# Nine gathered rows for every eight value tiles instead of ten, rows ahead of activations, and two value tiles loaded early, in a one-layer encoder kernel

## What is computed

```python
def _peer(h, w_q, subkeys, u_tab, v_tab):
    q = (xt @ w_q).reshape(t, PEER_HEADS, 2, PEER_QDIM // 2)
    scores = jnp.einsum('thpd,hpkd->thpk', q, subkeys)
    ...
    experts = jnp.take_along_axis(cand_i, sel, axis=-1)   # 128 picks a token
    gates = jax.nn.softmax(top_s, axis=-1)
    def block(args):
        xb, eb, gb = args
        act = jax.nn.gelu(jnp.einsum('tkd,td->tk', u_tab[eb], xb), approximate=False)
        return jnp.einsum('tk,tkd->td', (gb * act), v_tab[eb])

h = _layer_norm(ALPHA * h + mix, ln1_g, ln1_b)
h = _layer_norm(ALPHA * h + ffn, ln2_g, ln2_b)
```

## Time and profile before

| | us |
|---|---|
| three runs | 1959.45, 1963.38, 1967.93 |
| median | 1963.38 |
| the profiled execution | 1959.66 |
| its span, first to last instruction | 1957.9 |
| TensorE busy | 1913.0 (98%) |
| VectorE busy | 1346.7 (69%) |
| GpSimd busy | 1402.1 (72%) |
| ScalarE busy | 986.1 (50%) |

### The profile page before, as it was taken

How to read it: one execution, slowest core, us unless ns; L and a number is a source line. 1 busy time by engine, 2 the same in 40 slices (tenths; PEclk the granted TensorE clock), 3 DMA queues, 4 the chain that set the end, 5 groups by cost and what they waited for, 6 DMA issues and landing times.

```text
span 1957.9 us, 34249 instructions
## 1 busy us (share of the span) xinstructions
PE 1913.0 (98%) x10830; PEld 1670.2 (85%) x10830; DVE 1346.7 (69%) x2302; ACT 986.1 (50%) x1518; POOL 1402.1 (72%) x962
## 2 busy tenths in 40 slices
PE   9999999998999999999999999999899999999996
PEld 8999888888998888888888888888788878778884
DVE  1744012214688878755899989997788888888866
ACT  4544434435445556566455544455455554555553
POOL 6877878886878889898788778784666666566101
PEclk9999999999999999999999999999999999999998
DMA  9555657567869888677877777776899999989881
GB/s 296 172 151 166 205 153 222 180 209 184 207 153 203 186 192 190 167 186 186 248 174 172 177 169 175 170 172 226 317 331 344 340 329 348 366 330 341 298 297 68
DMA packets 178777, 440.59 MB, mean 225 GB/s; under 512 B 27328, under 2 KB 38464, under 8 KB 160912
## 3 DMA queue, kind: packets, MB, share of 16 engines
q1 hardware_dynamic: 163280, 384.52, 68.0%
q0 software_dynamic: 14416, 50.61, 7.4%
q10 hardware_dynamic: 1008, 4.52, 0.6%
HBM read 426.79 MB, written 12.78 MB: 225 GB/s over the span
## 4 chain that ended last, share of the span: by engine, by line
PE 67%; POOL 10%; issue 8%; DMA 7%; DVE 4%; ACT 2%; SPq 2%; DVEq 1%; POOLq 0%; ACTq 0%
PE ps L1771 22%; PE ps L1729 14%; PE ps L1730 7%; PE ps L1469 6%; PE ps L1471 6%; PE ps L1470 6%; POOL u_lo L1398 6%; DMA v_raw<-in_peer_v 4%; POOL w_lo L1360 4%; PE ps L1711 3%; DMA u_raw<-in_peer_u 2%; DVE u_t L1040 1%; DVE v_lo L1265 1%; DVE far_sum L1250 1%; PE ps L1585 1%
## 5 line engine op out<-in xcount | busy, mean ns | idle before, releaser
L1398 POOL TENSOR_TENSOR u_lo<-u_t,u_hi 128x512 fp32r<-128x512 f32 x512 | 653.0, 1300 | 127.4 <-ACT u_hi L637 124.8
L1729 PE MATMUL ps<-xT,u_hi 128*128 128x512 f32 x2048 | 723.0, 397 | 0.5 <-POOL u_lo L1398 0.4
L1730 PE MATMUL ps<-xT,u_lo 128*128 128x256 f32 x2048 | 571.2, 279 | 0.0
L1360 POOL TENSOR_TENSOR w_lo<-raw,w_hi 128x1024 fp32r<-128x1024 f32 x174 | 430.9, 2490 | 110.0 <-ACT w_hi L506 101.1
L637 ACT ACTIVATE u_hi<-u_t 128x512 fp32r<-128x512 f32 x512 | 320.9, 632 | 350.1 <-DVE u_t L1040 349.9
L1729 PEld LDWEIGHTS ps<-xT,u_hi 128*128 128x128 f32 x2048 | 384.3, 188 | 88.2 <-issue 0.9
L1040 DVE STREAM_TRANSPOSE u_t<-u_raw 128x512 f32<-128x512 f32 x512 | 354.1, 700 | 94.7 <-PE ps L1730 51.1
L1730 PEld LDWEIGHTS ps<-xT,u_lo 128*128 128x128 f32 x2048 | 386.1, 189 | 0.0
L506 ACT ACTIVATE w_hi<-raw 128x1024 fp32r<-128x1024 f32 x175 | 184.8, 1059 | 277.7 <-PE ps L1471 258.8
L1771 PE MATMUL ps<-v_hi,m_hi 128*128 128x512 f32 (+1 forms) x896 | 280.4, 380 | 18.1 <-DVE m_lo L1269 11.3
L1771 PE MATMUL ps<-v_hi,m_lo 128*128 128x512 f32 (+1 forms) x896 | 276.5, 376 | 0.0
(11 more groups left out here) (224 smaller groups left out, 2659.3 us busy)
## 6 DMA issues: line engine op xcount, KB each, us to landing
u_raw<-in_peer_u SPq DMA_DIRECT2D x512, 256.0 KB, 4.8
v_raw<-in_peer_v SPq DMA_DIRECT2D x126, 1024.0 KB
raw<-in_w_in SPq DMA_DIRECT2D x111, 512.0 KB, 3.7
raw<-in_w_out SPq DMA_DIRECT2D x32, 512.0 KB, 3.8
raw<-in_w_peer_q SPq DMA_DIRECT2D x128, 128.0 KB, 5.5
act_dram<-act_w ACTq DMA_DIRECT2D x4, 1024.0 KB, 6.7
act_dram<-far_act SPq DMA_DIRECT2D x64, 64.0 KB, 5.1
x_again<-in_x SPq DMA_DIRECT2D x1, 2048.0 KB, 8.0
```

Source lines behind the costliest of these rows:

```text
L1360: pool.tensor_tensor(w_lo[:, k, :], raw[:, k, :], w_hi[:, k % HI_RING, :].bitcast(F32), ALU.subtract).then_inc(lo_done, 1)
L1398: pool.tensor_tensor(u_lo[:, r, :], u_t[:, r, :], u_hi[:, r, :].bitcast(F32), ALU.subtract).then_inc(ulo_done, 1)
L1729: pe.matmul(acc, u_hi[:, r, c], xT[:, :, kt, :], start=kt == 0, stop=False)
L1730: ins = pe.matmul(acc[:, 0:T], u_lo[:, r, c], xT_hi[:, kt, :], start=False, stop=kt == KT - 1)
```

## The change

Four things are done.

1. The first norm's gain and shift are loaded in four halves of 0.5 MB, one behind every second step of the last `w_out` group, and no longer between the subkeys and the query weights.
2. The picks go nine for every eight tiles: five in one four of tiles, four in the next. They run from tile 8 to tile 121. GpSimd first gathers five rows, then asks for the gates, then gathers nine activations; after that one row and one activation in turn. The indices are loaded without waiting for the far stores; VectorE waits for the gates alone (`gate_in`). A row has to wait until the row four (or, for a part of the slots, five) before it is added.
3. Tiles 126 and 127 are loaded as four halves beside value tiles 74 to 77, and are split by ScalarE and VectorE between tiles 120 and 123. `ln2g_sb` is loaded behind tile 125, the last value load.
4. For the last four tiles TensorE takes 126, 127, 124, 125 in each bank. ScalarE and VectorE split half 0 of 124 and 125 first, then half 1 of both.

```diff
-S_CHUNK, S_FIRST = 5, 2
+S_CHUNK, S_FIRST = (5, 4), 2
+S_PAIR = sum(S_CHUNK)
+S_SLOTS = S_CHUNK[0]
...
+            for k in range(STEPS):
+                load_step(O_END - 1, k, w_out[0], (O_END - 1 - B_END) * COL)
+                if k % 2:
+                    dst, row, c = (ln1g_sb, ln1_g, half_row(k // 2)) if k < 4 else (ln1b_sb, ln1_b, half_row(k // 2 - 2))
+                    sp.dma_start(dst[:, c], row[0:1, c].to_broadcast([P, HALF])).then_inc(ln1_rows_in, 16)
...
-            sp.dma_start(ln1g_sb[:], ln1_g[0:1, :].to_broadcast([P, D])).then_inc(ln1_rows_in, 16)
-            sp.dma_start(ln1b_sb[:], ln1_b[0:1, :].to_broadcast([P, D])).then_inc(ln1_rows_in, 16)
...
+                elif n < 10:
+                    t, h = divmod(n - 6, 2)
+                    sp.dma_start(v_late_raw[:, n - 6, :], v_rows[P - 2 + t][:, half_row(h)]).then_inc(v_late, 16)
...
             for s in range(4):
-                v_high(P // 4 - 1, s, 1, last=True)
+                v_high(P // 4 - 2, s, 1)
+                if s % 2 == 0:
+                    v_high_late(s // 2)
+            act.wait_ge(far_added, 1)
+            for s in range(2):
+                act.wait_ge(v_in[s], P // 4 * 16)
+                act.activation(v_hi_end[:, 2 * s, :], v_raw[:, 2 * s, :], ACT.Copy).then_inc(v_hi_done, 1)
+                m_high(m_hi4[:, s, :], P - 4 + s, 1, m_hi_done)
+            for s in range(2):
+                act.activation(v_hi_end[:, 2 * s + 1, :], v_raw[:, 2 * s + 1, :], ACT.Copy).then_inc(v_hi_done, 1)
...
+            def row_gather(k):
+
+                n, j = divmod(k, S_PAIR)
+                if j >= S_SLOTS:
+                    pool.wait_ge(row_added, k - S_SLOTS + 1)
+                elif n:
+                    pool.wait_ge(row_added, k - S_CHUNK[1] + 1)
...
             pool.wait_ge(spread_mm, P - U_SPREAD)
             pool.wait_ge(hot_done, P - U_SPREAD)
+            pool.dma_start(sp_at[:].rearrange("p s k -> p (s k)"), at_dram).then_inc(picks_in, 16)
+            pool.wait_ge(near_out, 64)
+            pool.wait_ge(picks_in, 16)
+            pool.wait_ge(uparts_free, UR + 4 * P)
+            for k in range(S_SLOTS):
+                row_gather(k)
             for s in range(2):
                 pool.wait_ge(far_out[s], 16 * P // 4)
...
-            act_gather(0)
-            act_gather(1)
-            for n in range(S_END):
-                row_gather(n)
-                if n + 2 < S_END:
-                    act_gather(n + 2)
+            pool.dma_start(sp_gate[:], gate_dram).then_inc(gate_in, 16)
+            for k in range(S_PAIR):
+                act_gather(k)
+            for k in range(S_SLOTS, P):
+                row_gather(k)
+                if k - S_SLOTS + S_PAIR < P:
+                    act_gather(k - S_SLOTS + S_PAIR)
...
-                    for s in range(4):
-                        if a == 0 and b % 2 == 0:
-                            pe.wait_ge(v_lo_done, 2 * (P - 4 + s) + b // 2 + 1)
-                        ins = v_products(s, b // 2, a, last=True, stop=s == 3, cs=(b % 2,))
+                    for s in (2, 3, 0, 1):
+                        if a == b == 0 and s >= 2:
+                            pe.wait_ge(late_lo, s - 1)
+                        elif a == 0 and b % 2 == 0 and s < 2:
+                            pe.wait_ge(v_lo_done, 2 * (P - 4) + b + s + 1)
+                        ins = v_products(s, b // 2, a, last=True, stop=s == 1, cs=(b % 2,))
```

More of the change, by code:

```diff
@@ L1256, in weights, with m_low @@
                 dve.tensor_tensor(sp_w[:, k], sp_w[:, k], sp_gate[:, k], ALU.mult)
[L1258 to L1263 removed]
+            def m_low(ml, mh, i, half, done):
+                dve.tensor_tensor(by_four(ml), tile_w(half, i - P // 2 * half), by_four(mh.bitcast(F32)), ALU.subtract).then_inc(done, 1)
@@ L1278, in _, with v_low_added @@
             dve.memset(far_sum[:], 0.0)
[L1279 removed]
+            dve.wait_ge(gate_in, 16)
             for s in range(4):
                 v_low(1, s, 0)
[L1283 to L1286 removed]
+            def v_low_added(n, h, half):
+                weights(n, h, S_CHUNK[h])
                 for s in range(4):
[L1288 removed]
@@ L1301, in _ @@
-            dve.scalar_tensor_tensor(far, far, float(ALPHA), far_sum[:], ALU.mult, ALU.add).then_inc(far_added, 1)
-            for ii in range(S_FIRST + S_END, P // 4 - 1):
-                for s in range(4):
-                    v_low(ii, s, 1)
-            for s in range(4):
-                v_low(P // 4 - 1, s, 1, last=True)
+                    v_low(S_FIRST + n * 2 + h, s, half, added=[(n, h * S_CHUNK[0] + c) for c in range(S_CHUNK[h]) if c * 4 // S_CHUNK[h] == s])
+            for half in range(2):
+                with dve.Fori(half * (S_PAIRS // 2), (half + 1) * (S_PAIRS // 2)) as n:
+                    for h in range(2):
+                        v_low_added(n, h, half)
```

179 lines of the change are left out of this document (88 added, 91 removed).

## The result

| kernel | median us | lowest to highest | before beside it | ratio, 95% interval |
|---|---|---|---|---|
| changed | 1938.18 | 1934.55 to 1941.25 (4 runs) | 1965.22 | 0.9866 [0.9836, 0.9895] |
| changed, again | 1940.82 | 1935.10 to 1948.13 (6 runs) | 1965.52 | 0.988 [0.9858, 0.9902] |

What follows compares the result with a forecast made beforehand. TensorE's own work was taken as the value stretch's bound, with 26 us above it winnable by order. Gains of 5.2 + 5.0 + 1.0 + 7.6 = 18.8 off 1959.66, plus 3.7, gave 1944.6 us, range 1936 to 1955.

Steps and rivals of the forecast that it cites:

- The seam: Before the first query matmuls: moving the first norm's gain rows brings subkeys and TensorE sooner, with clock 5.2 us gained.
- The start: Tile 8 of the value stretch: rows gathered before activations remove wait, slow clock and restart, 6.5 less 1.5, net 5.0.
- The crowding: Value tiles 2 to 4: early rows sharing DMA delay tile 2, late far stores delay the gates; 1.5 us cost.
- The middle: Between tile 8 and the last four tiles: nine picks in eight tiles shorten short waits, net 1.0 us gained.
- I let the 7.5 fall to 4.5: Waits away from the six loads beside value tiles: assumed to fall from 7.5 to 4.5 us, bounds 0 and 7.5.
- ten loads in a row: Ten value tiles with another load beside each: lose 4 us at 413 GB/s, where six gave 3.
- tiles 120 to 123: Just ahead of the last four tiles: VectorE's 6 more splits and two additions cost 1 us.
- A floor: Value stretch: TensorE's undisturbed time per tile, taken as 4.48 us from twelve tiles in 53.80 us.
- The last four tiles: End of the value stretch: 126 and 127 first, so no wait and no slow clock; 7.6 us gained, bounds 4.6 and 7.6.
- Larger: Rival: all 7.5 us of waits between go and no crowding comes, 1938.6 us; chance 0.12.
- The lower ceiling: Rival: DMA gives 358 GB/s, not 413, over ten crowded tiles; gain 15, 1948.3 us; chance 0.05.

Runs made afterwards that it cites:

- the runs: Changed kernel with the old seam, the old GpSimd start, the old last-four-tiles order, then all three undone: 1939.80, 1940.16, 1946.55, 1955.05 us.
- The edit undone: Changed kernel with the last four tiles in their own order, splits too, 126 and 127 still loaded early: 1946.55 us, ratio 0.9925.
- the sum above: Four changed-kernel runs, three parts undone singly and together, solved as adding: gain 25.0 us, of which seam 4.1, start 4.4, end 10.8, rest 5.7.

## Why the prediction was right, and where not

*The sign and most of the size were right*: 1938.2 and 1940.8 against 1944.6, inside 1936 to 1955. What fell short is one term.

*The seam*, 5.2: 5.1 us by the traces, from the subkeys' turn to the first score (44.1 us in eight traces, 48.8 to 50.3 in six, so 4.7 to 6.2), and 4.1 by the runs. Right, with its clock.

*The start*, 6.5 gained less 1.5: no wait at tile 8, 1.16 to 1.74 us at tile 4 in all six executions of this start, 4.4 net by the runs against 5.0. Right, though a part of its size is the execution's: the same old order cost 0 to 4.58 us of waits at tile 8. The crowding hit the load of tile 4, issued among the rows, and the gates, where the sum had tile 2 in mind. The Trainium skill (DMA: Bandwidth & Descriptors, Queues, rings and completion order) says that a DMA engine goes round its queue rows packet by packet, and by that tile 2 was to be 2 to 3 us late. The trace doesn't show it for tile 2 (ScalarE's wait 2.55 us, 2.70 before). It would fit tile 4, which ScalarE could start 11 us after its load was issued; but in the kernel before, too, single value loads on the critical chain took 6.7 to 11.8 us.

*The middle*, net 1.0, was the mis-sized term: 5.7 us by the runs. The step that failed is "I let the 7.5 fall to 4.5 ... since nothing in the trace gives a law for it". The trace had one: 11 of the 14 waits stood at tiles with two additions, most of them with the chain just shown. I had counted that tiles with two additions halve, and priced the waits by megabytes. Away from the extra loads (outside 1641 to 1695 us) the waits behind tile 8 add up to 5.65 and 6.35 us in the two traces of before, and to 2.04 and 0.65 in those of the changed kernel; the forecast left more than half of them standing. Two of that term's parts were nearer: ten loads in a row do lose 4 us of waits and once 1.7 of clock (4 predicted), at 392 GB/s where 413 was used; and nothing was lost in tiles 120 to 123 beyond 0.3 us (1 predicted). A floor 2 us too high (a tile at 4.48 us, where the stretch without waits gives 553.9 from its first matmul) hid some of what could be won.

*The last four tiles*, 7.6: 25.5 to 17.9 us, no wait, full clock. The mechanism is right, the size partly luck, since the second trace of the kernel before gives 4.6 (22.5 to 17.9). The edit undone gives 7.0 us between the traces with and without the order, 5.7 to 8.4 between the medians (1946.55 against 1940.8 and 1938.2), 10.8 by the sum above. Of the three ways the traces are the ones that see only this place, each in one execution; the other two carry the scatter of the rest.

*The execution.* The sum was made against an execution 3.7 us under its median, and the 3.7 were added to the forecast. Both profiled executions of before lie at the low end of their runs (1959.66 of 1959.45 to 1967.93, 1958.70 of 1958.70 to 1969.09), those of the changed kernel don't. So the medians lie further apart than the profiled executions, 27.0 us against 18.4 in the first comparison and 24.7 against 18.8 in the second, and no trace shows where those 6 to 9 us lie in the kernel before; this stays open.

*The rivals.* Larger (1938.6) is the nearest in time, and half for the reason it named: most waits between went, but the crowding it left out was there (tile 4). The lower ceiling falls; its terms also give a gain of 16.1 us, not the 15 put down. The Trainium skill (DMA: Bandwidth & Descriptors, Bandwidth) puts the HBM side at about 358 GB/s, and in the same section calls that each core's part with both cores of the HBM domain streaming. Here one core runs, and 392 GB/s over 50 us stand against it as a ceiling; the measurement decides.

## What to carry to other kernels

When an engine waits a little and often, lay the waits over the program's period before pricing them: here they stood every fourth tile, and pointed at work placed between the input and the result that the next engine asks for. Put work that nobody waits for behind the last result of a step, not between its steps; in the kernel before that alone gave as much as most of this change. Gathers that take turns, and loads spread over many tiles, cost less here than the same bytes in blocks; for the gathers the reason is open. And profile a kernel twice before pricing a loss by one trace: the same code lost 7.6 us in its last four tiles once and 4.6 the next time.

## What was not expected of the hardware

- Rate: one core's loads moved 392 GB/s over 50 us (share 0.99) and 413 over 9 us.
- With gathers in blocks, ScalarE and SP both went on some 5 us after TensorE's rows end the tile whose release they wait for (1578.25 and 1578.29 against 1572.97). No run shows why.
- A 1 MB value load takes very different times: 6.7 to 11.8 us on the critical chain of the kernel before, 7.38 in the earlier trace rows.
- GpSimd waited 3.5 us for the gates' small load in one execution and 5.6 in another, of kernels with the same start, and tile 8 was waited for only in the second.
- The granted clock fell to 0.50 (the lower level) after single waits of TensorE of 1.84, 1.86, 2.55 and 3.13 to 7.85 us, but not after ones of 1.83 and 2.23 in other kernels. After the same 1.64 us in the last four tiles of the kernel before and its variants it stood at 0.50 for 6.8 us, for 3.4, or not at all. The length of a single wait does not tell whether it falls.
